# Constant matmuls into an unused PSUM bank at the norms and the head norm of a two-layer decoder step

## What is computed

```python
def rmsnorm(x, g):
    return x * rsqrt(mean(x * x, -1) + RMS_EPS) * g

for i in range(2):
    up, us = rmsnorm(xp, norm_mix[i]), rmsnorm(xs, norm_mix[i])
    mk, mv = mem_kv(mem_prompt, norm_mem[i], w_mem_kv[i])     # rmsnorm, then a projection
    # layer 0: mLSTM heads, h = h * rsqrt(mean(h * h, -1) + RMS_EPS) * head_g  (the head norm)
    # layer 1: native sparse attention over paged rows
    # both: 4 heads of cross attention over mk, mv
    x = x + concat(heads, memory_heads) @ w_out[i]
    x = x + swiglu(rmsnorm(x, norm_ffn[i]))                    # layer 0, dense
    x = x + moe_swiglu(rmsnorm(x, norm_ffn[i]))                # layer 1, top 2 of 8 experts
y = rmsnorm(x, norm_final)
```

## Time and profile before

| | before |
|---|---|
| median of 3 runs | 1975.97 us (1974.4 to 1978.47) |
| the profiled execution: its own time | 1977.16 us |
| its span in the trace | 1975.4 us |
| TensorE busy (matmul) | 1851.0 us, 94% |
| VectorE busy | 1315.7 us, 67% |
| ScalarE busy | 922.1 us, 47% |
| TensorE clock granted, mean | 0.95 of full |

### The profile page before, as it was taken

One profiled execution on the slowest core, in us unless ns is written; L12 is line 12 of the kernel. 1 busy time (PEld: TensorE's weight loads), 2 busy tenths in 40 slices (PEclk: granted clock), 3 DMA queues, 4 the chain that ended last, 5 costly groups with the idle time before them and its releaser, 6 DMA issues.

```text
span 1975.4 us, 27858 instructions
## 1 busy us (share of the span) xinstructions
PE 1851.0 (94%) x10214; PEld 1493.7 (76%) x10214; DVE 1315.7 (67%) x1741; ACT 922.1 (47%) x1241; POOL 71.8 (4%) x104
## 2 busy tenths in 40 slices
PE   7999987999999999999988888999999999999994
PEld 4666656999874487777755676888888888888883
DVE  4542776887533456778642444888888888888885
ACT  2222220000011135767455215778787778787772
POOL 0100010000110000000000001000000000000001
PEclk9998978999999979999889788999999999999997
DMA  5622535675783233333769345999999999999992
GB/s 178 203 86 61 114 94 179 224 266 169 200 282 118 80 133 108 114 121 129 257 242 357 143 145 186 365 382 393 374 370 369 378 394 372 370 366 376 388 381 94
DMA packets 198371, 472.15 MB, mean 239 GB/s; under 512 B 12499, under 2 KB 78287, under 8 KB 196890
## 3 DMA queue, kind: packets, MB, share of 16 engines
q1 hardware_dynamic: 189698, 428.77, 60.6%
q0 software_dynamic: 8576, 42.11, 6.7%
HBM read 455.81 MB, written 29.78 MB: 246 GB/s over the span
## 4 chain that ended last, share of the span: by engine, by line
PE 75%; DVE 5%; issue 3%; ACT 2%; DMA 1%; SPq 1%; POOLq 0%; POOL 0%; DVEq 0%; ACTq 0%
PE bank L2405 68%; PE bank L2408 7%; ACT arena L2952 1%; SPq L2260 1%; DMA arena<-in_cache_nsa 1%; DVE arena L1564 1%; DVE uT L2674 0%; DMA ring<-in_cache_nsa 0%; ACT ring L2952 0%; DMA ring<-scr_y,mem_all 0%; DVE rtmp L2670 0%; DVE ring L1991 0%; DVE uT L1564 0%; DVE ring L1979 0%; DVE arena L1502 0%
## 5 line engine op out<-in xcount | busy, mean ns | idle before, releaser
L2405 PE MATMUL bank<-arena_r 128*128 128x448 f32 (+2 forms) x3176 | 775.5, 357 | 12.7 <-DVE uT_r L672 10.1
L2405 PEld LDWEIGHTS bank<-arena_r 128*128 128x128 f32 x3176 | 584.4, 189 | 72.9 <-DVE uT_r L672 10.5
L1871 DVE TENSOR_TENSOR ring_r<-ring,arena_r 128x1792 fp32r<-128x1792 f32 (+1 forms) x216 | 436.0, 2048 | 48.4 <-ACT arena_r L2952 47.0
L2952 ACT ACTIVATE arena_r<-ring 128x1792 fp32r<-128x1792 f32 (+1 forms) x216 | 368.9, 1726 | 137.1 <-PE bank L2405 117.8
L2952 ACT ACTIVATE arena<-bank 64x256 f32<-64x256 f32 (+11 forms) x419 | 177.8, 434 | 380.8 <-PE bank L2405 211.3
L2405 PE MATMUL bank<-arena 128*128 128x256 f32 (+18 forms) x1518 | 258.3, 357 | 9.4 <-ACT arena L2952 4.0
L2405 PE MATMUL bank<-ring_r,arena_r 128*128 128x448 f32 (+1 forms) x840 | 246.1, 374 | 0.0
L2405 PEld LDWEIGHTS bank<-arena 128*128 128x128 f32 (+10 forms) x1518 | 174.5, 171 | 66.3 <-issue 39.3
L1871 DVE TENSOR_TENSOR arena_r<-arena,arena_r 128x1792 fp32r<-128x1792 f32 (+1 forms) x72 | 138.4, 1935 | 57.2 <-ACT arena_r L2952 55.8
L2405 PEld LDWEIGHTS bank<-ring_r,arena_r 128*128 128x128 f32 x840 | 157.7, 188 | 21.9
L2405 PE MATMUL bank<-arena_r,ring_r 128*128 128x264 f32 x528 | 151.0, 286 | 0.0
(11 more groups left out here) (378 smaller groups left out, 1661.0 us busy)
## 6 DMA issues: line engine op xcount, KB each, us to landing
ring<-in_w_moe_gu SPq DMA_DIRECT2D x144, 896.0 KB, 7.1
ring<-in_w_moe_d SPq DMA_DIRECT2D x60, 1024.0 KB, 7.3
ring<-in_cache_nsa SPq DMA_DIRECT2D x176, 256.0 KB, 4.6
arena<-in_w_moe_gu SPq DMA_DIRECT2D x48, 896.0 KB, 6.9
ring<-in_w_ffn_gu SPq DMA_DIRECT2D x22, 1024.0 KB, 7.2
arena<-in_cache_nsa SPq DMA_DIRECT2D x80, 256.0 KB, 5.8
ring<-in_w_in_a SPq DMA_DIRECT2D x8, 1536.0 KB, 6.5
arena<-in_w_moe_d SPq DMA_DIRECT2D x12, 1024.0 KB, 7.4
```

The source lines that it names most:

```text
L1871: V.tensor_tensor(unit_low(c), unit_slot(c), unit_high(c), ALU.subtract).then_inc(S("m_sp"), 1)
L2405: return nc.tensor.matmul(out, lhsT, rhs, start=first, stop=last, **kw_)
L2952: return nc.scalar.activation(out, in_, fn, **kw_)
```

## The change

A helper `keep_busy(b, n)` issues `n` matmuls that multiply `ones` (128x128) by the first 512 columns of `consts` into bank `b`. Nobody reads the result, and they signal nothing. It is called in six spots: 8 of them behind `norm(0)`; 8 ahead of the head sums and 6 behind them; 5 ahead of `norm(2)` and 20 behind it; 12 behind `norm(4)`. That makes 59. The wait for `mt_ev` is moved up, ahead of the first 8, since it guards their bank.

```diff
-        def layer_b_pe(pe, mm, tr, got, norm):
+        def layer_b_pe(pe, mm, tr, got, norm, keep_busy):
...
             norm(4, NT)
+            keep_busy(6, 12)
 
 
             pe.wait_ge(S("ld_wr"), 16)
...
+            def keep_busy(b, n):
+
+                for _ in range(n):
+                    mm(bank[b][:, :], ones, consts[:, 0:512])
+
             def norm(n, width):
...
                 m = mm(bank[0][:, 0:NMEM], ones, mem_sq[:, k, :], k == 0, k == KT - 1)
             m.then_inc(S("nrm_mm"), 1)
 
+            pe.wait_ge(*done("mt_ev", 9))
+            keep_busy(1, 8)
             pe.wait_ge(S("nrm_out"), 1)
             w = got("gxa")
-            pe.wait_ge(*done("mt_ev", 9))
...
+            keep_busy(7, 8)
             for h in range(MH):
                 pe.wait_ge(*done("hsq0" if h < 6 else "hsq"))
                 m = mm(bank[0][0:MH, 0:NT], csel[0:MD, h, :], sq[0:MD, h, :], h == 0, h == MH - 1)
             m.then_inc(S("hn_mm"), 1)
+            keep_busy(7, 6)
             pe.wait_ge(*done("den"))
             pe.wait_ge(S("c_ev"), 8)
             pe.wait_ge(S("hn_rs"), 1)
...
+            keep_busy(6, 5)
             norm(2, NT)
+            keep_busy(6, 20)
             pe.wait_ge(*done("u_split0"))
...
-            layer_b_pe(pe, mm, tr, got, norm)
+            layer_b_pe(pe, mm, tr, got, norm, keep_busy)
```

## The result

| | before | the change |
|---|---|---|
| median of 20 runs each | 1976.88 us (1974.13 to 1990.66) | 1991.1 us (1977.84 to 2002.41) |
| ratio, 95% interval | | 1.0071 (1.0053 to 1.0089) |
| the profiled execution: its own time, its span | 1977.16, 1975.4 us | 1994.79, 1993.0 us |

The change makes the kernel slower, by 10 to 18 us; 8.6 were forecast. TensorE's program is the same but for the added matmuls, so the two traces can be laid side by side: at each stretch I give how much later the same instruction starts ("offset"). The helper `mm` is line 2406 now, `tr` is 2409, ScalarE's line is 2963; in the experiments' kernels the numbers differ by a line or a few.

What follows compares the result with a forecast made beforehand. TensorE, busy 1851.0 of 1975.4 us, was taken to bound the kernel. The terms 0.65 + 6.85 - 5.2 + 5.5 + 0.8 = +8.6 us on the 1975.97 median gave 1984.5 us, range 1979.0 to 1991.0.

Steps and rivals of the forecast that it cites:

- Price of one matmul: Each added float32 matmul is two records and costs 0.856 us at the high clock; all 59 are 50.5 us.
- The rival built on half the price: One record per matmul, 0.43 us each: only the eight ahead of the head sums cost, 1965 us; chance 0.05 including 216 ns.
- Step 1: First norm, eight matmuls ahead of the gates: loss 2.45, gain 1.8 at full clock, sum +0.65 us.
- Step 2: Ahead of the head sums, no wait to fill: all eight matmuls lie on the path, +6.85 us, nothing absorbs it.
- Step 3: Behind the head sums, six matmuls: loss 1.9, gain 7.1 in broadcasts and first projection block, sum -5.2 us.
- Step 4: Around norm(2), five and twenty matmuls: loss 7.85, gain 2.35 in the feed-forward, sum +5.5 us.
- Step 5: Behind norm(4), twelve matmuls: loss 3.7, router gain 2.9 from bounds 0 and 5.0, sum +0.8 us.
- the second rival: Clock stays up through the transposes, 2.1 us back, and shifted low stretches elsewhere give 2.5: 1980 us; chance 0.09.
- what the prediction named as a sign that it is wrong: Added matmul at 0.43 us, idle time behind those at norm(2), or far stretches changing clock by more than a few us.

Runs made afterwards that it cites:

- experiment 9: The change with all 59 matmuls, each moving 256 columns of the constants instead of 512: 1975.99 us, ratio 0.9989 to the kernel before.
- experiments 1: The change with its counts cut to 4, 0, 3, 3, 11 and 7 to fit the waits: 1971.37 us, ratio 0.9951 to the kernel before.
- experiment 6: The fitted counts plus 3 matmuls at the seventh head and 3 at the start of layer 1: 1965.81 us, ratio 0.9923 to the kernel before.

## Why the prediction was right, and where it was off

The sign and the reason hold: the groups are too long for their waits, and the kernel pays for it. The size came out at +14.2 us by the medians, against +8.6. The 1991.1 us lie at the upper edge of the range, 0.1 us above 1991.0 as it stands and inside it once the kernel before is taken at the 1976.88 us of these runs instead of 1975.97. That the range holds it is owed to its width, not to the mechanism alone: in the profile the five steps sum to 11.4 us, and another 6.2 arise where no step looked.

- **Price of one matmul, 0.856 us, two records: right.** 0.43 us between records; experiment 9 shows that it goes by columns. The rival built on half the price is refuted by the same rows. The 216 ns that the Trainium skill, "TensorE: Matmul & The Clock Gate", section "Back-to-back issue gap", gives for 512 columns are not the price of a float32 matmul in this trace, which is 856 ns.
- **Step 1, +0.65: right** (+0.8).
- **Step 2, +6.85 and nothing hidden: right,** a little short: +7.5 in the profile, since the first of the eight started at the low clock, and 7.06 us in the profile of the eight alone. Taking them out of the change gave back 5.4 us by the medians.
- **Step 3, 1.9 - 7.1: mis-sized.** The loss was 2.2. The gain was 5.0 in the change's profile and 3.2 to 5.0 with the fitted counts (experiments 1 and 6), because the clock fell behind the broadcasts or early in the first block, with TensorE busy. The broadcasts have only 8 partitions as input; that this is the reason fits, but no run separates it. I had let the clock stay up through 3.6 us of them and the 3.55 us behind. The matmuls that move 2 columns had warned me of work that doesn't hold the clock, and I didn't apply them here.
- **Step 4, +5.5: right,** in the change's profile (+5.5) and alone (+5.5 in the profile, 6 by the medians).
- **Step 5, +0.8 with bounds: right in sum** (+0.4 in the change, 0 alone), with other parts: in the change the router and the transposes saved 5.9 us, which the second rival had, and 2.5 were lost behind them.
- **The rest of the kernel: missing.** The second rival let low stretches elsewhere change and priced them only in its favour; my own sum put them at nothing, without a reason. In this profile they cost 6.2 us net (with 0.3 at the program's ends), and the runs spread over 25 us. The kernel before is less steady than the "2 us either way" that I started from: 19 of its 20 runs lie within 7.5 us, and single ones reach 1991 to 1996. Against what the prediction named as a sign that it is wrong, stretches far from the four places did change their clock by more than a few us. That the spread of the change is larger was measured; what causes it is open.

The likeliest correction to the forecast is thus +2.4 for step 3, +0.7 for step 2, and some 3 us by the medians (6 in this profile) for the stretches that nobody edited.

## What to carry to other kernels

Filling a wait with throwaway matmuls pays only where they end before the wait does: price them by the starts of records of the same shape and type in your own trace, and leave a group out where TensorE arrives with its inputs about to be ready. With the counts fitted, the same idea that cost 14 us gained 6 to 10, and with two more waits 12 to 15 (by medians and by ratios). After such an edit compare all stretches by clock, not only the edited ones, and take a median of many runs, since one profile can be 5 us off either way.

## What the runs showed of the hardware

- A busy TensorE does not hold its clock by being busy: behind 3.77 us of broadcasts with 8 partitions of input the clock was at 0.53 for the next 7.2 us of matmuls with 96. In experiment 6 it fell only during that block, which took 5.52 us. It fits that before, behind the waits, the clock was up again 3.75 us into the gates and 5.13 us into the feed-forward, but at 0.50 for 13.70 us from the start of the broadcasts. The stretch in the fitted version:

```profile
276.16:283.40 7.24, 7.24 (x18) 5.63 (x18) 6.96 (x9) 0.00 (x0) 0.55 (x1) 0.53 0.12 41
```

- Constants that are mostly zeros hold the clock: it was at 1.00 behind the groups around norm(2) and at the gates (the stretches of 34.16 and 352.30 above).
- The 24 transposes can run at the high clock throughout: 2.84 us in the change, 4.95 and 5.38 where it was low for part or all of them. The Trainium skill, "TensorE: Matmul & The Clock Gate", section "Part 4: PE-mode transpose", says that the full clock does not engage for transposes; here it stayed up through 2.84 us of them behind 10.46 us of added matmuls and 4.12 us of the router, and the row of 1196.79 to 1203.60 has 1.00. Whether transposes alone would raise it, no run shows.
- One program's runs fall into groups 3 to 12 us apart (1962, 1969 and 1972 with the fitted counts; 1983 and 1995 with both groups at the head norm), while the mean granted clock goes with them: 0.957, 0.955 and 0.952 in the first case.
